# Attention scores as three rounded fp32r products in place of one fp32 product, with the rests made by DVE and the row of maxima rounded by GpSimd

## The reference, cut to what matters

```python
def attend(q_nope, q_rope, q_pos, k_nope, k_rope, v, k_pos):
    s = (jnp.einsum("bqhd,bkhd->bhqk", q_nope, k_nope)
         + jnp.einsum("bqhr,bkr->bhqk", q_rope, k_rope)).astype(jnp.float32) * SM_SCALE
    allowed = (k_pos[None, :] // CHUNK) <= (q_pos[:, None] // CHUNK)
    s = jnp.where(allowed[None, None], s, jnp.finfo(jnp.float32).min)
    p = jax.nn.softmax(s, axis=-1).astype(v.dtype)
    return jnp.einsum("bhqk,bkhd->bqhd", p, v)
```

## Time and profile before

| | value |
|---|---|
| median of 3 runs | 1430.45 us (1429.91 to 1431.16) |
| profiled execution, its own time | 1430.73 us |
| its span | 1429.0 us, mean granted clock 0.989 |
| PE busy | 1382.4 us, 97% of the span |
| DVE busy | 889.3 us, 62% |
| ACT busy | 441.3 us, 31% |
| POOL busy | 27.8 us, 2%, 29 instructions |
| chain that ended last | PE 88%, DVE 7%, ACT 1%, issue 1% |
| scores and values in that chain | L1034 5%, L1015 5% |

### The profile page before, as it was taken

The page is one execution under the profiler, slowest core; times in us unless marked ns, Lnnn a source line. Parts: engine busy times, 40 slices in busy tenths (PEclk is TensorE's granted clock), DMA queues, the critical chain, the costliest instruction groups (busy, mean ns, idle before and its releaser), DMA issues.

```text
span 1429.0 us, 23512 instructions
## 1 busy us (share of the span) xinstructions
PE 1382.4 (97%) x9500; PEld 1275.6 (89%) x9500; DVE 889.3 (62%) x1442; ACT 441.3 (31%) x713; POOL 27.8 (2%) x29
## 2 busy tenths in 40 slices
PE   7899999999999999999799999999999999999997
PEld 3599999999997555579699999999999999999996
DVE  7788778464563345568965555556565555656566
ACT  4521110123401344346642323132232323132323
POOL 0000000000002011000000000000000000000000
PEclk9999999999999999999899999999999999999999
DMA  9344444611212332010012112111102112121103
GB/s 367 97 133 133 133 133 103 244 38 46 86 29 56 110 102 65 9 30 16 1 60 60 55 34 73 30 58 44 59 29 59 47 41 73 29 59 44 59 30 122
DMA packets 112933, 107.06 MB, mean 75 GB/s; under 512 B 9544, under 2 KB 97184, under 8 KB 112112
## 3 DMA queue, kind: packets, MB, share of 16 engines
q1 hardware_dynamic: 110272, 105.05, 24.3%
q10 hardware_dynamic: 2608, 1.28, 0.3%
HBM read 88.89 MB, written 9.88 MB: 69 GB/s over the span
## 4 chain that ended last, share of the span: by engine, by line
PE 88%; DVE 7%; ACT 1%; DMA 1%; issue 1%; SPq 1%; DVEq 0%
PE PS L1124 31%; PE PS L1142 16%; PE PS L728 16%; PE PS L1034 5%; PE PS L1015 5%; PE PS L894 4%; PE PS L1072 1%; PE PS L1223 1%; PE PS L827 1%; PE PS L781 1%; PE PS L967 1%; DVE ACC L1808 1%; PE PS L987 1%; DMA ADA<-in_w_ada 1%; PE PS L922 1%
## 5 line engine op out<-in xcount | busy, mean ns | idle before, releaser
L2217 DVE TENSOR_TENSOR EL<-HALF_W,EH 128x512 fp32r<-128x512 f32 x175 | 120.3, 688 | 132.1 <-ACT EH L1543 131.0
L1124 PE MATMUL PS<-HBH_T,EH 128*128 128x264 f32 x704 | 188.9, 288 | 9.7 <-issue 3.8
L1124 PE MATMUL PS<-HBL_T,EH 128*128 128x264 f32 x704 | 188.8, 288 | 0.0
L1543 ACT ACTIVATE EH<-HALF_W 128x512 fp32r<-128x512 f32 x175 | 109.4, 626 | 256.1 <-PE PS L1142 151.3
L2340 DVE SCALAR_TENSOR_TENSOR X<-PS,MOD,X 128x792 f32<-128x792 f32 (+2 forms) x240 | 125.4, 578 | 70.2 <-PE PS L1142 70.2
L1142 PE MATMUL PS<-AL,EH 128*128 128x264 f32 x640 | 162.7, 285 | 0.0
L1142 PE MATMUL PS<-AH,EH 128*128 128x264 f32 x640 | 162.3, 284 | 0.0
L728 PE MATMUL PS<-HH,WH 128*128 128x352 f32 x456 | 149.3, 328 | 0.5 <-DVE WL L1825 0.5
L728 PE MATMUL PS<-HL,WH 128*128 128x352 f32 x456 | 147.7, 325 | 0.0
L1124 PE MATMUL PS<-HBH_B,EH 128*128 128x264 f32 x528 | 141.1, 287 | 3.7 <-DVE EL L2217 2.7
L1124 PE MATMUL PS<-HBH_T,EL 128*128 128x264 f32 x704 | 144.3, 286 | 0.0
(11 more groups left out here) (287 smaller groups left out, 2583.2 us busy)
## 6 DMA issues: line engine op xcount, KB each, us to landing
ADA<-in_w_ada SPq DMA_DIRECT2D x22, 1024.0 KB, 5.4
HALF_W<-in_w_gate SPq DMA_DIRECT2D x22, 512.0 KB, 3.9
HALF_W<-in_w_up SPq DMA_DIRECT2D x22, 512.0 KB, 3.9
HALF_W<-in_w_down SPq DMA_DIRECT2D x22, 512.0 KB, 3.8
RAW<-in_w_in SPq DMA_DIRECT2D x20, 512.0 KB, 6.2
x_saved_rows<-X SPq DMA_DIRECT2D x2, 2112.0 KB, 12.3
X<-x_saved_rows SPq DMA_DIRECT2D x4, 1056.0 KB, 6.6
out<-ORW SPq DMA_DIRECT2D x8, 512.0 KB, 2.6
```

Of the source, the lines that this page charges most:

```text
L1124: mm = pe.matmul(PS[:, 2 * s + n, 0:HQ], w, x[:, k, n * HQ:(n + 1) * HQ], start=(first and w is wh and x is xh), stop=(ends and w is wl), ...
L1543: act.activation(dst if len(src.shape) == 2 else dst.rearrange("p (k c) -> p k c", k=2), src, ACT.Copy)\
L2217: dve.tensor_tensor(el, src, eh.bitcast(F32), ALU.subtract).then_inc(entry_lo, 1)
```

## The change

The scores become three fp32r products each: `KTH*QTH + KTH*QTL + KTL*QTH` over all 105 partitions. POOL rounds a head's operands into two alternating buffers (`QTH`, `KTH` by h % 2). A new DVE function `rest_head(h)` makes `QTL` and `KTL` in place of `QT` and `KT`, after `keep_maxima(h)`: 96 x 1056 and 64 x 1312 elements, for heads 0 to 2 also the nine partitions of mask and maxima (9 x 1056), and `KT` over 105 partitions. The row of maxima now lands in a buffer `QTM` of its own, with the mask, and a new POOL function `round_maxima(h)` rounds its nine partitions into `QTH`; `scores(h, 0)` waits for this and for the rests. `round_head(h)` now runs after `round_maxima(h-1)` and after all scores of head h-2. The sample's maxima also use the rounded operands. `QT`'s nine last partitions are zeroed (three memsets). The new buffers lie where `X` comes back to, so two of its four loads are issued only after the last scores. `BIG`, the mask's size, goes from 1e30 to 2^100. In the diff, semaphore declarations and the constant `OWN = NOPE + ROPE` are left out.

```diff
         KT = [at(f"KT{b}", [P, TK], F32, o + 5248 * b) for b in range(3)]
-        KTH = at("KTH", [P, TK], F32R, o + 15744)
-        QTH = at("QTH", [P, T], F32R, o + 20992)
+        KTL = [at(f"KTL{b}", [P, TK], F32R, o + 5248 * b) for b in range(3)]
+        KTH = [at("KTH0", [P, TK], F32R, o + 15744), at("KTH1", [P, TK], F32R, 8 * U - 5248)]
+        QTH = [at("QTH0", [P, T], F32R, o + 20992), at("QTH1", [P, T], F32R, 7 * U - 5248)]
+        QTL = [at("QTL0", [P, T], F32R, o + 25216), at("QTL1", [P, T], F32R, o + 25216 + U),
+               at("QTL2", [P, T], F32R, 8 * U + 24576)]
+        QTM = at("QTM", [P, T], F32, 4 * U)
         QT = [at("QT0", [P, T], F32, o + 25216), at("QT1", [P, T], F32, o + 25216 + U),
...
                     sp.wait_ge(s_full, STEPS * (h - 2))
-                    sp.wait_ge(m_full, STEPS * (h - 2))
-                    sp.wait_ge(rounded, 2 * (h - 2))
                 sp.dma_start(QT[b][0:NOPE, :], QN[NOPE * e:NOPE * (e + 1), j, :]).then_inc(assembled[b], 16)
...
-                b = h % 3
                 sp.wait_ge(m_kept, h + 1)
-                sp.dma_start(QT[b][PLAIN:CONTRACT, 0:S].rearrange("o (t q) -> o t q", t=KD),
-                             MROW[0:KD, h % 2, :]).then_inc(max_rows[b], 16)
-                sp.dma_start(QT[b][PLAIN:CONTRACT, S:T], MROW[KD:KD + 1, h % 2, 0:SD]).then_inc(max_rows[b], 16)
+                if h >= 1:
+                    sp.wait_ge(max_rounded, h)
+                sp.dma_start(QTM[PLAIN:CONTRACT, 0:S].rearrange("o (t q) -> o t q", t=KD),
+                             MROW[0:KD, h % 2, :]).then_inc(max_rows, 16)
+                sp.dma_start(QTM[PLAIN:CONTRACT, S:T], MROW[KD:KD + 1, h % 2, 0:SD]).then_inc(max_rows, 16)
             load_key_rows(0)
             assemble(0)
-            sp.wait_ge(key_ends_set, 3)
+            sp.wait_ge(key_ends_set, 6)
             load_key_rows(1)
             load_key_rows(2)
+            sp.wait_ge(q_full, NJ)
+            sp.dma_start(QTM[OWN:PLAIN, :], c_qmask).then_inc(key_rows_loaded, 16)
             assemble(1)
...
                     .then_inc(aw_loaded[n], 16)
+            def load_x(a, b):
+
+                sp.dma_start(X[:, a:b, :], XS[:, a:b, :]).then_inc(x_back, 16)
+
             for h in range(HEADS):
                 if h + 1 < HEADS:
                     load_maxima(h + 1)
                 if h + 3 < HEADS:
                     assemble(h + 3)
-                if h < KH:
+                if h < 2:
                     if h == 0:
-                        sp.wait_ge(q_full, NJ)
                         sp.wait_ge(x_saved, 32)
-                    sp.dma_start(X[:, 2 * h:2 * h + 2, :], XS[:, 2 * h:2 * h + 2, :]).then_inc(x_back, 16)
+                    load_x(2 * h, 2 * h + 2)
+            sp.wait_ge(s_full, STEPS * HEADS)
+            sp.wait_ge(max_rounded, HEADS)
+            load_x(KH, KH + 2)
+            load_x(KH + 2, KD)
...
                             bank = 6 + c // 512 if t >= 4 else 6 + (t + 1) % 2
-                            mm = pe.matmul(PS[:, bank, 0:w], QTH[0:PLAIN, t * P:(t + 1) * P],
-                                           KTH[0:PLAIN, c:c + w], start=True, stop=True)
+                            mm = pe.matmul(PS[:, bank, 0:w], QTH[h % 2][0:PLAIN, t * P:(t + 1) * P],
+                                           KTH[h % 2][0:PLAIN, c:c + w], start=True, stop=True)
                     else:
-                        mm = pe.matmul(PS[0:SD, 6, 0:PAST + SD], QT[h % 3][0:PLAIN, S:T], KT[h % 3][0:PLAIN, S:TK],
+                        mm = pe.matmul(PS[0:SD, 6, 0:PAST + SD], QTH[h % 2][0:PLAIN, S:T], KTH[h % 2][0:PLAIN, S:TK],
                                        start=True, stop=True)
...
                 if i == 0:
-                    pe.wait_ge(max_rows[h % 3], 32 * (h // 3 + 1))
-                    pe.wait_ge(assembled[h % 3], 64 * (h // 3 + 1))
+                    pe.wait_ge(max_rounded, h + 1)
+                    pe.wait_ge(head_lo, 2 * (h + 1))
                 if n >= 2:
                     pe.wait_ge(exp_done, n - 1)
                 else:
                     pe.wait_ge(k_kept_dve, 2)
                     pe.wait_ge(k_kept_act, 2)
+                kh, kl, qh, ql = (x[0:CONTRACT, :] for x in (KTH[h % 2], KTL[h % 3], QTH[h % 2], QTL[h % 3]))
                 if i < KD:
                     q0 = P * i
                     for c in range(0, S - q0, 512):
                         w = min(512, S - q0 - c)
-                        mm = pe.matmul(PS[:, b + c // 512, 0:w], KT[h % 3][0:CONTRACT, q0:q0 + P],
-                                       QT[h % 3][0:CONTRACT, q0 + c:q0 + c + w], start=True, stop=True)
+                        for part, (k, q) in enumerate(((kh, qh), (kh, ql), (kl, qh))):
+                            mm = pe.matmul(PS[:, b + c // 512, 0:w], k[:, q0:q0 + P], q[:, q0 + c:q0 + c + w],
+                                           start=(part == 0), stop=(part == 2))
                 else:
                     for m in range(3):
                         col, r = key_tile(KD + m)
-                        mm = pe.matmul(PS[0:r, b, SD * m:SD * (m + 1)], KT[h % 3][0:CONTRACT, col:col + r],
-                                       QT[h % 3][0:CONTRACT, S:T], start=True, stop=True)
+                        for part, (k, q) in enumerate(((kh, qh), (kh, ql), (kl, qh))):
+                            mm = pe.matmul(PS[0:r, b, SD * m:SD * (m + 1)], k[:, col:col + r], q[:, S:T],
+                                           start=(part == 0), stop=(part == 2))
                 mm.then_inc(s_full, 1)
...
                 if h >= 2:
-                    dve.wait_ge(max_rows[(h - 2) % 3], 32 * ((h - 2) // 3 + 1))
+                    dve.wait_ge(max_rows, 32 * (h - 1))
                 dve.tensor_copy(MROW[0:STEPS, h % 2, :], PS[0:STEPS, 7, 0:P]).then_inc(m_kept, 1)
+
+            def rest_head(h):
+
+                b = h % 3
+                dve.wait_ge(rounded, 2 * h + 2)
+                dve.tensor_tensor(QTL[b][0:OWN, :], QT[b][0:OWN, :], QTH[h % 2][0:OWN, :].bitcast(F32), ALU.subtract)\
+                    .then_inc(head_lo, 1)
+                if h < 3:
+                    ends = QT[b][OWN:CONTRACT, :]
+                    dve.tensor_tensor(QTL[b][OWN:CONTRACT, :], ends, ends, ALU.subtract)
+                k = CONTRACT if h < 3 else NOPE
+                dve.tensor_tensor(KTL[b][0:k, :], KT[b][0:k, :], KTH[h % 2][0:k, :].bitcast(F32), ALU.subtract)\
+                    .then_inc(head_lo, 1)
...
             keep_values(10)
+            rest_head(0)
             keep_keys(2)
             for h in range(HEADS):
                 if h + 1 < HEADS:
                     for n in range(STEPS):
                         maxima(h + 1, n)
                     keep_maxima(h + 1)
+                    rest_head(h + 1)
                 if h >= 2:
...
             pool.wait_ge(max_zeroed, 1)
-            pool.memset(KT[0][NOPE + ROPE:CONTRACT, :], -1.0).then_inc(key_ends_set, 1)
+            pool.memset(KT[0][OWN:CONTRACT, :], -1.0).then_inc(key_ends_set, 1)
+            pool.memset(QT[0][OWN:CONTRACT, :], 0.0).then_inc(key_ends_set, 1)
             pool.wait_ge(key_rows_loaded, 16 * 4)
             def round_head(h):
                 pool.wait_ge(assembled[h % 3], 64 * (h // 3 + 1))
+                if h >= 2:
+                    pool.wait_ge(s_full, STEPS * (h - 1))
+                    pool.wait_ge(max_rounded, h)
+                q, k = (CONTRACT, CONTRACT) if h < 2 else (OWN, NOPE)
+                pool.tensor_copy(QTH[h % 2][0:q, :], QT[h % 3][0:q, :]).then_inc(rounded, 1)
+                pool.wait_ge(rounded, 2 * h + 1)
+                pool.tensor_copy(KTH[h % 2][0:k, :], KT[h % 3][0:k, :]).then_inc(rounded, 1)
+
+            def round_maxima(h):
+
+                pool.wait_ge(rounded, 2 * max(h, 1) + 2)
                 if h >= 1:
-                    pool.wait_ge(m_full, STEPS * h)
-                pool.tensor_copy(QTH[0:PLAIN, :], QT[h % 3][0:PLAIN, :]).then_inc(rounded, 1)
-                pool.tensor_copy(KTH[0:PLAIN, :], KT[h % 3][0:PLAIN, :]).then_inc(rounded, 1)
+                    pool.wait_ge(max_rounded, h)
+                pool.wait_ge(max_rows, 32 * (h + 1))
+                pool.tensor_copy(QTH[h % 2][OWN:CONTRACT, :], QTM[OWN:CONTRACT, :]).then_inc(max_rounded, 1)
...
             for b in range(1, 3):
-                pool.memset(KT[b][NOPE + ROPE:CONTRACT, :], -1.0).then_inc(key_ends_set, 1)
+                pool.memset(KT[b][OWN:CONTRACT, :], -1.0).then_inc(key_ends_set, 1)
+                pool.memset(QT[b][OWN:CONTRACT, :], 0.0).then_inc(key_ends_set, 1)
             pool.wait_ge(q_full, NJ)
             pool.wait_ge(rows_turned, UNITS)
             pool.wait_ge(lat_copied, 32)
-            pool.wait_ge(key_ends_set, 3)
+            pool.wait_ge(key_ends_set, 6)
             pool.memset(V[:, :, :, VH:2 * VH], 1.0).then_inc(ones_kept, 1)
             pool.wait_ge(ones_kept, 1)
-            pool.wait_ge(key_rows_loaded, 16 * 12)
```

(16 more changed lines are left out.)

## The result

The changed kernel takes 1442.86 us (median of 4 runs, 1440.66 to 1444.74), the kernel before 1430.81 in the same comparison: a ratio of 1.0081, 95% interval 1.0066 to 1.0096. It is 12 us slower, and 7 us above the range that was forecast. The profiled execution took 1443.55 with a span of 1441.8, 12.8 above the span of before, at a mean granted clock of 0.979 against 0.989.

A forecast was written before the change was run, and what follows sets the result against it. PE was taken to bound the heads: seven boundaries x -0.21 = -1.5, head 0 -0.67, head 7 -0.53, DVE +2.1, first two rests +0.14, together -0.5 us: 1429.9. Range 1428 to 1432.5; for 8 in 10, 1427.0 to 1435.5.

The forecast's parts named there:

- the new wait at the head boundary: PE waits 0.70 us for POOL's cast at each of seven head boundaries, turning -0.91 a period into -0.21.
- its first rival: POOL and DVE block each other at the first two boundaries and h = 3 and 5: +4.7, 1434.6 us; chance 0.28.
- POOL's cast of the row: At the head boundaries, POOL casts the 1056 columns of maxima in 1.07 us, starting 0.08 after landing.
- some 0.07 behind POOL, 0.14 in all: At the first two boundaries, DVE's nine-partition rests end at T0 + 4.26, against POOL's T0 + 4.19.
- The sum without the port: Whole kernel with no blocking of POOL and DVE: -0.5 us together, 1429.9 against the median.
- The landing: DMA of the maxima at head boundaries lands 2.0 us after issue, with bounds of 1.5 and 2.47.
- the sample's nine products: Short products of the sample's scores cost 9 x 0.09 = 0.81 us against 0.54, +0.27 a period.
- the other heads can't be far below their 2.2: Landing of the maxima: one head of seven took 2.47 us, the others were taken as near their bound of 2.21.
- DVE's rests and reciprocals: Reciprocals queued behind the rests at h = 2 and 4 make 1.0 us of new wait, twice: +2.1.
- Rates: PE's three fp32r products against one fp32: first scores 1.72 to 1.40 us, second 1.70 to 1.44.
- The third and fourth tiles: PE's shorter scores there (1.29 to 1.06, 1.08 to 1.02) gain nothing, as DVE's chain of reductions runs beside them.
- Loads of X: Two late loads, issued at 625.6 and needed at 638.30, take 11.7 us one behind the other: 637.3, hidden.

The follow-up runs named there:

- the filled kernel: Changed kernel plus two useless fp32 matmuls of 384 columns on PE ahead of the first scores of heads 1, 2, 4 and 6: 1430.02 us.
- the kernel with both apart: Changed kernel, but DVE's output scaling at heads 3 and 5 waits for POOL's cast, nine-partition rests for heads 1 and 2 made ahead: 1425.96 us.
- the fastest kernel: Changed kernel with DVE's copy rounding the maxima, no POOL between landing and scores, and DVE's rests and reciprocals spread to other places: 1419.75 us.
- the dense kernel: Changed kernel with DVE's copy rounding, POOL memsets replacing the cast (three at heads 1, 2, 4, 6), and two fp32 products ahead of those waits: 1442.5 us.
- the kernel of one product: Fastest complete kernel with only the high-by-high product of the scores' three, rests still made: 1412.99 us.

## Why the prediction was wrong

The step that failed is the price of the new wait at the head boundary. The forecast counted a wait of PE at its own length (0.70 each), and its first rival did so too ("Four times 1.14 and a little for the turns, +4.7"). At four boundaries of the changed kernel PE stands still for 1.45 to 1.67 us and soon after is at half clock for 6.8, which costs about 3 us more each time. The prediction names the clock once, as 1.00 in the heads; none of its cases asks what a new wait does to it.

A second step of the forecast itself failed as well: it took POOL's cast of the row at 1.07 everywhere, and at four heads DVE holds it to 2.16 to 2.34. This case was among the rivals. Without the clock it would have stayed inside the range: the filled kernel takes 1430.02. That this is next to the forecast's 1429.9 is luck, since 4.4 for the hold and DVE's third pass, of which the forecast had 0.14, are set off by some 4 that it had too much at the boundaries.

By its own steps:

*The port.* The mechanism of the first rival was right to the place: heads 1, 2, 4 and 6, by the third pass at the first two and by the scaling at the others. Its price was about right as well. Filled and apart, the four long periods differ by 1.25, 1.28, 0.93 and 0.96, 4.4 us together, against 4 x 1.14 plus turns. Some 0.8 of the 4.4 is not the hold but DVE's third pass at the first two boundaries: "some 0.07 behind POOL, 0.14 in all" was forecast, and with the shorter landing it is 0.4 each. Its chance of 0.28 was too low: an overlap of 0.15 by rough ends was let stand against a stated rule. The rule of the Trainium skill (SBUF — State Buffer, "Who interferes with whom") is borne out with its detail, that the reading is held and not a pure write: 2.34 for a copy, 0.97 for a memset.

*The clock.* 11.9 us, in no case of the prediction. With those 4.4 it makes 16.3; the changed kernel is 16.9 above the kernel with both apart, and the remaining 0.6 is within what these medians can tell. What the runs show is that the length of a wait alone doesn't decide, and that what stands around it does: boundary waits of 1.25 to 1.67 us among short products bring the clock down, of 1.25 and 1.70 behind dense ones don't, of 2.13 and 2.30 do even there; and the wait of 1.44 which was harmless behind dense values is not at 1.23 behind nine short products. The windows are those of one profile for each kernel; the medians of the runs go with them. Where the edge lies stays open.

*The sum without the port.* The forecast 1429.9 stands against 1425.96 for the kernel kept apart, 4 us too slow. The mis-sized term is the wait at the boundaries: a period without reciprocals is 19.66, 0.83 less than before, where -0.21 was forecast. The landing took 1.66 instead of 2.0, first scores starting 3.99 after the copy and not 4.52, so the wait is 0.4 and not 0.70. PE is there at 3.58 (483.80 less the copy at 480.22 in the fastest kernel), not 3.82, since the sample's nine products take 0.67 and not 0.81 and the eighth tile 0.29, not 0.32. Six heads had given only an upper bound, 2.21, and the step "the other heads can't be far below their 2.2" doesn't follow from it. The 2.47 of the seventh was the exception, though landings of 2.50 and 2.70 came at head 2 of the filled and of the dense kernel.

*DVE's rests and reciprocals.* 1.0 us of new wait at h = 2 and 4 was forecast, 1.02 and 1.05 are measured over the period of 19.66. *Rates.* 1.40 for the first scores and 1.42 for the second were forecast as 1.40 and 1.44. *The third and fourth tiles.* Nothing gained there, as forecast: from the end of the first maxima to the end of the third 3.92 us (468.23 to 472.15), with the second reduction in the chain between.

*Loads of X.* They are issued at 637.04, and the first addition starts at 649.58, 12.5 after; before, the last scores and it were as far apart. Hidden, as forecast; they land 5.0 and 7.3 us after their issues, so the 11.7 for one behind the other was too long.

## What to carry to other kernels

A new wait of TensorE isn't priced by its length alone: look at the granted clock behind the longest waits of a trace and at what stands around them, and if a long one stands among small matmuls, put dense work next to it, even useless work, or move it to where the engine is dense. Before a GpSimd instruction is put on the way to TensorE, list VectorE's passes with two SBUF inputs at that time; the two hold each other. A rounding that an existing copy can do needs no instruction, and no engine, of its own.

## What the runs showed of the hardware that had not been expected

- The granted clock fell to 0.50 (1.2 GHz) for 3.4 to 6.8 us behind waits of PE of 1.2 to 1.7 us next to products of 32 columns, and stayed at 1.00 behind waits of 1.25 to 1.70 that followed dense ones. One fall stood behind a wait of 0.79. In the kernel of one product, where PE waits again and again, a fall at 500.0 stood behind waits of 0.84, 0.57 and 0.31 us (486.99, 490.32, 497.57), and one from 541 on lasted 10 us.
- DVE's passes are stretched by POOL's casts as well, and not only those with two SBUF inputs: the one-input cast of 1056 columns went from 0.71 (before, at 586.39) to 1.47.
- A memset of POOL, untouched by the third pass at 0.97, took 1.43 at 553.48 in the kernel with the dense work, where DVE's cast of 1056 columns ran until 553.99 and was stretched to 1.31. What holds a write there wasn't followed further.
- A 32-column fp32r product with its own weight load took 0.67 / 9 = 0.074 us, less than the 0.09 of an fp32 record.
